# The order of ScalarE's and VectorE's work in a recurrent stage: weight splits ahead of the convolution

## The chip, the core and the metric

The kernel runs on one NeuronCore of a Trainium2 chip (trn2). TensorE multiplies matrices, VectorE and ScalarE do elementwise work, GpSimd some reductions and transfers, SyncE issues most weight transfers. The metric is the device time of one execution in microseconds (us), median over several executions. Lower is better.

## The reference

The model has four residual sub-layers over a sequence of 1024 tokens with 1024 channels: a pooling mixer, a dense MLP, an mLSTM mixer and a second MLP. The change lies in the mLSTM mixer:

```python
proj = jnp.einsum('bsd,de->bse', h, w_in)          # q, k, v, o and two gates
qk = jax.nn.silu(causal_depthwise_conv(qk, conv_w, conv_b))   # 4 taps
...
def mlstm_chunk_step(carry, inp):
    C, n, m = carry
    ...
    s = jnp.einsum('bhtd,bhsd->bhts', q, k) * jnp.exp(log_d - m_out[..., None])
    num = jnp.einsum('bhts,bhsd->bhtd', s, v) + inter[..., None] * jnp.einsum('bhtk,bhkv->bhtv', q, C)
    ...
    C_new = decay[..., None, None] * C + jnp.einsum('bhs,bhsk,bhsv->bhkv', wts, k, v)
...
hs = hs * lax.rsqrt(jnp.mean(hs * hs, axis=-1, keepdims=True) + RMS_EPS)
gated = jax.nn.sigmoid(o_pre) * hs * head_norm_w
return jnp.einsum('bsd,de->bse', gated, w_out)
```

There are 8 heads of 128 channels. Everything is float32.

## The kernel before, in words

**Matmuls in three passes.** Each float32 weight block is split into a high part, rounded to the format that TensorE takes at full rate (`w_hi`, made by ScalarE, `split_hi`, line 1211), and the remainder (`w_lo`, made by VectorE from `raw` and `w_hi`, `split_lo`, line 1739). A product is then three matmuls: high by high, high by low, low by high (lines 778 to 780). The weights and their parts have little room: `raw` holds two blocks, `w_hi` and `w_lo` also two blocks of 1024 columns. So the split of block n overwrites block n - 2, and ScalarE waits in `split_hi` until the projection that used block n - 2 has ended (`group_done`, `BEFORE`), and for the transfer of the raw block. SyncE issues the transfer of block n once block n - 2 is split in both parts.

**The recurrent stage** (755 to 1345 us of the trace) works on the sequence in two halves of 512 tokens, and on the 8 heads in each, 16 steps numbered j = 0 to 15, which are called head 0 to head 15 here. A head has four projections, `("head", j, t)`: q, k, v and the output gate, each 24 matmuls over 512 columns. TensorE's order is written out by hand in `lstm` (line 1074): projection 0 of head j, `turn(j - 1)` (transposes of k and v and the scores, lines 1029 to 1035), projection 1, `updates(j - 1)` (state updates, line 1046), projection 2, `numerators(j - 1)` (lines 1057 and 1061), projection 3, `turn_back(j - 1)` (transposes of the normed head `hnorm`, line 1071). So while head j is projected, head j - 1 is finished. Behind every four heads stands an output product (`second_product`, four blocks), at the start of heads 5, 9 and 13 and at the end.

**ScalarE and VectorE** each have a list of their own, also written by hand (`lstm` at lines 1506 and 2230), and work it off strictly in order; they meet at semaphores. Their pieces, for head j:

- `conv_input(j, t)` (ScalarE, lines 1569 and 1572): moves projection t out of its PSUM bank, scaled into `win` and plain into `craw`. `conv(j, t)` (VectorE, lines 2122 to 2128): the other three taps of the convolution.
- `query(j)` and `keys(j)` (ScalarE, lines 1481 and 1486): silu of the convolution, which makes `qT` and `kT`. `value_copy` (1464) and `output_gate` (1471) move projections 2 and 3.
- `decay_matrix(j - 1)` (ScalarE, 1592, with a load of the exp table): `mx_b`. `by_tokens(j - 1)` (1606 and 1609): `kw` and `v_tok`, which `updates` needs. `rows_to_all(j)` issues two small transfers.
- `probabilities(j - 1)` (VectorE, 2140): `prob`, from the scores and `mx_b`. `states(j - 1)` (2157): three intermediate states `mid`. `rows_for(j)` (2205, 2209). `denominators`, `normalize` (2169 to 2185): `hnorm`. `gate_head` (2194 to 2199).
- `head_squares` and `head_root` (ScalarE, 1619 and 1626).
- `tick(j, part)`: the background work of the slot 4j + part. It runs the normalisations of the layer before or of the other half: squares on ScalarE (1246), sums on VectorE (1799), a reciprocal (1744), residuals (1132 and 1811), normed tiles and their split. `LSTM_SLOTS` says what lies in which slot; heads 1 to 7 and 9 to 15 have the same pattern.
- `BLOCK["head", j, t] + 1` is the block behind projection t of head j: for t = 0 that of projection 1, and so on; for t = 3 that of head j + 1, or of the output product.

Of the kernel before, what the change touches and what calls it, by code (L numbers as in the profile page):

```python
# [20 lines left out]
HEADS = 8  # L21
# [206 lines left out]
def build(nc, x_in, x_tokens, weights, w_first, w_second, vecs_in, consts_in, bands_in, out):  # L228
# [9 lines left out]
    with ExitStack() as ctx:  # L238
# [962 lines left out]
        def _(act):  # L1201
# [286 lines left out]
            def first_head():  # L1488

                split_hi(BLOCK["gate", 0] + 1)  # L1490
                split_hi(BLOCK["head", 0, 0] + 1)
                gates(0)
                split_hi(BLOCK["head", 0, 1] + 1)
                conv_input(0, 0)
                conv_input(0, 1)
                split_hi(BLOCK["head", 0, 2] + 1)
                value_copy(0)
                split_hi(BLOCK["head", 0, 3] + 1)
                gate_weights(0)
                output_gate(0)  # L1500
                query(0)
                keys(0)
                tick(0, 2)
                tick(0, 3)

            def lstm():
                first_head()
                for j in range(1, STEPS + 1):
                    half = j // HEADS
                    g = heads_out(j)  # L1510
                    if g is not None:
                        for b in range(OUT_BLOCKS):
                            split_hi(BLOCK["out", g, b] + 1)
                            if g % 2 == 0:
                                for d in range(2):
                                    out_copy(g, 2 * b + d)
                    if j == STEPS:
                        decay_matrix(j - 1)
                        by_tokens(j - 1)
                        head_norm(j - 1)  # L1520
                        continue
                    if j % HEADS == 0:
                        split_hi(BLOCK["gate", half] + 1)

                    split_hi(BLOCK["head", j, 0] + 1)
                    if j % HEADS == 0:
                        gates(half)
                    if j % HEADS == 1:

                        act.wait_ge(rows_stored, 32 * (half + 1))  # L1530
                        rows_to_all(j - 1)
                    conv_input(j, 0)
                    for f in (by_tokens, decay_matrix) if j % HEADS == 1 else (decay_matrix, by_tokens):
                        f(j - 1)
                    tick(j, 0)
                    split_hi(BLOCK["head", j, 1] + 1)
                    query(j)
                    if j % HEADS:
                        rows_to_all(j)
                    tick(j, 1)  # L1540

                    conv_input(j, 1)
                    split_hi(BLOCK["head", j, 2] + 1)
                    keys(j)
                    value_copy(j)
                    head_squares(j - 1)
                    split_hi(BLOCK["head", j, 3] + 1)
                    head_root(j - 1)
                    tick(j, 2)
                    output_gate(j)  # L1550
                    if j % HEADS == 0:
                        gate_weights(half)
                    tick(j, 3)
                g = STEPS // FT - 1
                for b in range(OUT_BLOCKS):
                    split_hi(BLOCK["out", g, b] + 1)
                for k in range(KT):
                    post_square(5, k)
# [169 lines left out]
        def _(dve):  # L1728
# [487 lines left out]
            def first_head():  # L2216

                split_lo(BLOCK["gate", 0] + 1)
                gates(0)
                split_lo(BLOCK["head", 0, 0] + 1)  # L2220
                split_lo(BLOCK["head", 0, 1] + 1)
                gate_chain(0, lambda: split_lo(BLOCK["head", 0, 2] + 1))
                split_lo(BLOCK["head", 0, 3] + 1)
                conv(0, 0)
                conv(0, 1)
                gate_tail(0)
                tick(0, 2)
                tick(0, 3)

            def lstm():  # L2230
                dve.wait_ge(group_done, STEP[0, STEPS2 - 1][1])
                dve.memset(taps[:, :, :], 0.0)
                dve.memset(zrow[:, :], 0.0)
                dve.memset(m_run[:, 0:1], 0.0)
                dve.memset(rows[:, :], 0.0)
                dve.memset(state[:, :, :], 0.0)
                steps.finish(dve.memset(v_tok[:, :, HEAD_DIM:], 1.0))
                first_head()
                for j in range(1, STEPS + 1):
                    half = j // HEADS  # L2240
                    g = heads_out(j)
                    if g is not None:
                        take_out(g // 2, BLOCK["out", g, 0], GROUPS["out", g, 0], g % 2 == 0)
                    if j == STEPS:
                        probabilities(j - 1)
                        states(j - 1)
                        denominators(j - 1)
                        normalize(j - 1)
                        gate_head(j - 1)
                        continue  # L2250
                    if j % HEADS == 0:
                        split_lo(BLOCK["gate", half] + 1)
                        gates(half)
                    split_lo(BLOCK["head", j, 0] + 1)
                    conv(j, 0)
                    if j % HEADS == 1:
                        gate_columns(half)
                        rows_for(j - 1)
                    probabilities(j - 1)
                    tick(j, 0)  # L2260
                    split_lo(BLOCK["head", j, 1] + 1)
                    if j % HEADS == 0:
                        gate_chain(half, lambda: None)
                    states(j - 1)
                    tick(j, 1)
                    if j % HEADS == 0:
                        split_lo(BLOCK["head", j, 2] + 1)
                    conv(j, 1)
                    if j % HEADS:
                        split_lo(BLOCK["head", j, 2] + 1)  # L2270
                        rows_for(j)
                    denominators(j - 1)
                    split_lo(BLOCK["head", j, 3] + 1)
                    normalize(j - 1)
                    tick(j, 2)
                    gate_head(j - 1)
                    if j % HEADS == 0:
                        gate_tail(half)
                    tick(j, 3)
                g = STEPS // FT - 1  # L2280
                take_out(g // 2, BLOCK["out", g, 0], GROUPS["out", g, 0], g % 2 == 0)
                for k in range(KT):
                    chain_total(k, CHAIN_SUMS[5])
# [129 lines left out]
```

## Time and profile before

| | us |
|---|---|
| median of 3 runs | 2043.67 |
| lowest and highest | 2038.62 and 2045.17 |
| the profiled execution, its own time | 2044.57 |
| its span in the trace | 2042.8 |
| mean granted TensorE clock in it | 0.983 of full |
| TensorE busy in the span | 1950.9 |
| VectorE busy in the span | 1327.6 |
| ScalarE busy in the span | 1055.5 |

The trace is one execution. Matmuls overlap, so the start of one to the start of the next says more than the length of one. In brackets behind an instruction stands the idle time of its engine just before it, and who ended it by the profile; "issue" means that the profile names nobody. DVE is VectorE, ACT is ScalarE, PE is TensorE.

### The profile page before, as it was taken

Reading aid. Unit: us, or ns where it says so; the run is one execution under the profiler, and the core shown is the slowest. Engines: PE = TensorE matmul, PEld = TensorE weight load, DVE = VectorE, ACT = ScalarE, POOL = GpSimd, SP = SyncE. Lnnn points to the kernel's source line nnn. Section 1 sums busy time; section 2 is a strip of 40 time slices with the busy share of each in tenths; the row PEclk is TensorE's granted clock in tenths of the full one; section 3 lists DMA queues with packets and bytes.
Section 4 is the critical chain, followed back from the end, with each engine's and each line's share of the span. In section 5 each row is a group of like instructions: output and inputs, shape, how many; then the busy total and the mean of one; then the engine's idle time right before and its main releaser. Section 6 shows DMA issues by size and latency. Waiting matters only on the chain.

```text
span 2042.8 us, 24561 instructions
## 1 busy us (share of the span) xinstructions
PE 1950.9 (96%) x8652; PEld 1566.0 (77%) x8652; DVE 1327.6 (65%) x2073; ACT 1055.5 (52%) x1793; POOL 91.0 (4%) x121
## 2 busy tenths in 40 slices
PE   9999999998999999999999999899999999899996
PEld 7677788886888787778877778777778888688784
DVE  5675556555766877776767858676555655577765
ACT  6645454553444446766746756453555455344432
POOL 0020000000000200110000100020000000000110
PEclk9999999998999999999999999899999999899998
DMA  5254244349433533343223432243424336833453
GB/s 200 83 165 175 77 156 156 128 172 355 143 93 98 182 114 104 114 145 101 96 73 100 142 117 86 72 154 113 171 83 170 145 139 249 302 93 94 118 176 107
DMA packets 80569, 283.95 MB, mean 139 GB/s; under 512 B 9504, under 2 KB 9632, under 8 KB 73536
## 3 DMA queue, kind: packets, MB, share of 16 engines
q1 hardware_dynamic: 63424, 235.76, 33.1%
q0 software_dynamic: 8320, 27.27, 4.1%
q10 hardware_dynamic: 8704, 19.36, 3.1%
q8 instruction: 70, 1.15, 0.2%
q14 instruction: 51, 0.42, 0.1%
HBM read 213.08 MB, written 69.27 MB: 138 GB/s over the span
## 4 chain that ended last, share of the span: by engine, by line
PE 83%; DVE 6%; DMA 4%; ACT 4%; issue 3%; SPq 0%; POOL 0%; ACTq 0%; DVEq 0%
PE bank L778 7%; PE bank L780 7%; PE bank L779 6%; PE bank L995 4%; PE bank L997 4%; PE bank L996 4%; PE core L946 4%; PE core L947 4%; PE bank L946 4%; PE core L945 4%; PE bank L947 4%; PE bank L945 4%; PE core L995 4%; PE core L997 4%; PE core L996 4%
## 5 line engine op out<-in xcount | busy, mean ns | idle before, releaser
L1739 DVE TENSOR_TENSOR w_lo<-raw,w_hi 128x1024 fp32r<-128x1024 f32 x148 | 186.5, 1262 | 187.9 <-ACT w_hi L1211 185.9
L1211 ACT CAST w_hi<-raw 128x1024 fp32r<-128x1024 f32 x148 | 155.2, 1049 | 190.4 <-PE core L997 56.5
L1388 ACT CAST h_hi<-h_raw 128x512 fp32r<-128x512 f32 x178 | 110.2, 619 | 267.7 <-PE bank L997 112.8
L778 PE MATMUL bank<-x_hi,w_hi 128*128 128x512 f32 x560 | 227.9, 407 | 15.6 <-issue 14.9
L780 PE MATMUL bank<-x_hi,w_lo 128*128 128x512 f32 x560 | 222.2, 397 | 0.0
L779 PE MATMUL bank<-x_lo,w_hi 128*128 128x512 f32 x560 | 221.7, 396 | 0.0
L1988 DVE TENSOR_TENSOR h_lo<-h_raw,h_hi 128x512 fp32r<-128x512 f32 x178 | 122.6, 689 | 122.7 <-ACT h_hi L1388 122.3
L995 PE MATMUL bank<-h_hi,w_hi 128*128 128x512 f32 x424 | 170.9, 403 | 16.8 <-DVE h_lo L1988 16.8
L997 PE MATMUL bank<-h_hi,w_lo 128*128 128x512 f32 x424 | 170.4, 402 | 0.0
L996 PE MATMUL bank<-h_lo,w_hi 128*128 128x512 f32 x424 | 169.3, 399 | 0.0
L995 PE MATMUL core<-h_hi,w_hi 128*128 128x512 f32 x352 | 140.7, 400 | 7.5 <-DVE y L2049 7.5
L997 PE MATMUL core<-h_hi,w_lo 128*128 128x512 f32 x352 | 140.9, 400 | 0.0
L996 PE MATMUL core<-h_lo,w_hi 128*128 128x512 f32 x352 | 140.4, 399 | 0.0
L778 PEld LDWEIGHTS bank<-x_hi,w_hi 128*128 128x128 f32 x560 | 105.7, 189 | 42.7 <-issue 20.0
L1883 DVE TENSOR_TENSOR w_lo<-sums,w_hi 128x512 fp32r<-128x512 f32 x96 | 66.2, 690 | 101.5 <-ACT w_hi L1239 98.8
L780 PEld LDWEIGHTS bank<-x_hi,w_lo 128*128 128x128 f32 x560 | 105.5, 188 | 25.6
L779 PEld LDWEIGHTS bank<-x_lo,w_hi 128*128 128x128 f32 x560 | 105.6, 189 | 24.1 <-issue 1.0
L878 PE MATMUL bank<-x_hi,w_hi 128*128 128x512 f32 x256 | 105.1, 410 | 9.3 <-ACT y_part L1284 4.5
L995 PEld LDWEIGHTS bank<-h_hi,w_hi 128*128 128x128 f32 x424 | 81.4, 192 | 38.4 <-issue 10.2
L2027 DVE TENSOR_TENSOR w_lo<-w,w_hi 128x512 fp32r<-128x512 f32 x136 | 97.4, 716 | 9.4 <-ACT w_hi L1404 4.8
L1174 POOL PARTITION_ALL_REDUCE tot<-acc x10 | 34.5, 3454 | 1532.0 <-DVEq L1803 1532.0
L880 PE MATMUL bank<-x_hi,w_lo 128*128 128x512 f32 x256 | 101.7, 397 | 0.0
(314 smaller groups left out, 4487.1 us busy)
## 6 DMA issues: line engine op xcount, KB each, us to landing
raw<-weights SPq DMA_DIRECT2D x148, 512.0 KB, 3.4
h_pair_dram<-y SPq DMA_DIRECT2D x24, 1792.0 KB, 6.7
h_raw<-h_pair_dram SPq DMA_DIRECT2D x168, 256.0 KB, 2.8
w<-second_pairs SPq DMA_DIRECT2D x32, 768.0 KB, 8.1
x_scratch<-y POOLq DMA_DIRECT2D x48, 256.0 KB, 2.4
raw_odd<-first_pairs SPq DMA_DIRECT2D x12, 1024.0 KB, 7.3
raw<-first_pairs SPq DMA_DIRECT2D x12, 1024.0 KB, 7.1
xold<-x_scratch POOLq DMA_DIRECT2D x40, 256.0 KB, 3.6
```

Source lines behind the costliest of these rows:

```text
L778: nc.tensor.matmul(o, a, hi(t), start=(k == 0), stop=False)
L779: nc.tensor.matmul(o, a, lo(t), start=False, stop=False)
L780: last = nc.tensor.matmul(o, b, hi(t), start=False, stop=(k == n - 1))
L945: nc.tensor.matmul(o, a, xh[:, k, :], start=(fresh and k == 0), stop=False, skip_group_check=True)
L946: nc.tensor.matmul(o, a, xl[:, k, :], start=False, stop=False, skip_group_check=True)
L947: last = nc.tensor.matmul(o, b, xh[:, k, :], start=False, stop=(final and k == 3), skip_group_check=True)
L995: nc.tensor.matmul(o[:, :], a, hh, start=(fresh and first), stop=False, skip_group_check=True)
L996: nc.tensor.matmul(o[:, :], a, hl, start=False, stop=False, skip_group_check=True)
L997: ins = nc.tensor.matmul(o[:, :], b, hh, start=False, stop=(final and last), skip_group_check=True)
L1211: nc.scalar.copy(w_hi[:, ROW[u] * T:(ROW[u] + 2) * T], raw[:, (n % RAW) * BLK:(n % RAW + 1) * BLK]).then_inc(hi_ready, 1)
L1739: dve.tensor_tensor(w_lo[:, s], raw[:, (n % RAW) * BLK:(n % RAW + 1) * BLK], w_hi[:, s].bitcast(F32), ALU.subtract).then_inc(lo_ready, 1)
L1988: dve.tensor_tensor(lo, h_raw[:, at % H_RAW, :], hi.bitcast(F32), ALU.subtract).then_inc(h_lo_ready, 1)
```

## The change

In both lists, of ScalarE and of VectorE, the split of the block of projection 2 moves ahead of `conv_input(j, 0)` and `conv(j, 0)`, and that of projection 3 ahead of `conv_input(j, 1)` and `conv(j, 1)`: each stands at the place where the projection that held its rows has ended. The background work of the last slot, `tick(j, 3)`, moves from the end of head j to behind the split of projection 1 of head j + 1. On ScalarE `by_tokens` now comes ahead of `decay_matrix` in every head (before only where j % 8 = 1). In ScalarE's and VectorE's list:

```diff
@@ first_head() @@
                 tick(0, 2)
-                tick(0, 3)
@@ ScalarE, lstm() @@
                     if j == STEPS:
+                        tick(j - 1, 3)
                         decay_matrix(j - 1)
...
+                    tick(j - 1, 3)
+                    split_hi(BLOCK["head", j, 1] + 1)
                     conv_input(j, 0)
-                    for f in (by_tokens, decay_matrix) if j % HEADS == 1 else (decay_matrix, by_tokens):
-                        f(j - 1)
+                    by_tokens(j - 1)
+                    decay_matrix(j - 1)
                     tick(j, 0)
-                    split_hi(BLOCK["head", j, 1] + 1)
                     query(j)
                     if j % HEADS:
                         rows_to_all(j)
                     tick(j, 1)
 
+                    split_hi(BLOCK["head", j, 2] + 1)
                     conv_input(j, 1)
-                    split_hi(BLOCK["head", j, 2] + 1)
                     keys(j)
...
-                    tick(j, 3)
@@ VectorE, lstm() @@
                     split_lo(BLOCK["head", j, 0] + 1)
+                    tick(j - 1, 3)
+                    split_lo(BLOCK["head", j, 1] + 1)
                     conv(j, 0)
                     if j % HEADS == 1:
                         gate_columns(half)
                         rows_for(j - 1)
                     probabilities(j - 1)
                     tick(j, 0)
-                    split_lo(BLOCK["head", j, 1] + 1)
                     if j % HEADS == 0:
                         gate_chain(half, lambda: None)
                     states(j - 1)
                     tick(j, 1)
-                    if j % HEADS == 0:
-                        split_lo(BLOCK["head", j, 2] + 1)
+                    split_lo(BLOCK["head", j, 2] + 1)
                     conv(j, 1)
                     if j % HEADS:
-                        split_lo(BLOCK["head", j, 2] + 1)
                         rows_for(j)
...
-                    tick(j, 3)
```

TensorE's list is the same in both kernels.

On VectorE, in head 3, from `probabilities` on; `-` is the kernel before, `+` the changed one:

```order
 L2140 SCALAR_TENSOR_TENSOR prob<-core,mx_b 128x512
 L1744 RECIPROCAL rstd<-tot 128x512
-L1739 TENSOR_TENSOR w_lo<-raw,w_hi 128x1024
 L2157 SCALAR_TENSOR_TENSOR mid<-state,inter_b,core 128x129
 L2157 SCALAR_TENSOR_TENSOR mid<-mid,inter_b,core 128x129 x2
 L1132 SCALAR_TENSOR_TENSOR step_t<-y,vecs,rstd 128x512
 L1811 TENSOR_TENSOR y<-xold,step_t 128x512
-L2122 COPY craw<-taps 128x16
-L2123 COPY taps<-craw 128x16
-L2128 SCALAR_TENSOR_TENSOR win<-craw,vecs,win 128x512 x3
-L1739 TENSOR_TENSOR w_lo<-raw,w_hi 128x1024
+L1739 TENSOR_TENSOR w_lo<-raw,w_hi 128x1024
```

The first w_lo (projection 2) has moved up ahead of the first convolution, which ends just above this piece; the second one (projection 3) now stands ahead of the second convolution, whose three lines follow it in the changed kernel.

On ScalarE, in head 3, from `conv_input(3, 0)` to `query(3)`; the split of projection 2 now stands ahead of this piece:

```order
 L1569 ACTIVATE win<-bank,vecs 128x512
 L1572 COPY craw<-bank 128x512
+L1606 ACTIVATE kw<-core,cols 128x128 x4
+L1609 COPY v_tok<-core 128x4x128
 L1592 ACT_TABLE_LOAD
 L1592 ACTIVATE mx_b<-mx_b,cols 128x128 x4
-L1606 ACTIVATE kw<-core,cols 128x128 x4
-L1609 COPY v_tok<-core 128x4x128
-L1211 CAST w_hi<-raw 128x1024
 L1481 ACT_TABLE_LOAD
```

The split has left its place behind v_tok, and kw and v_tok stand ahead of the exp table and mx_b.

On VectorE, behind head 4, where four blocks of the output product and two of head 5 are split; acc is the sum of the background work of slot 19:

```order
 L2199 TENSOR_TENSOR hid_lo<-relu_sq,hid_hi 128x512
+L1739 TENSOR_TENSOR w_lo<-raw,w_hi 128x1024 x5
 L1799 TENSOR_TENSOR acc<-acc,sq 128x512 x2
-L1739 TENSOR_TENSOR w_lo<-raw,w_hi 128x1024 x5
+L1739 TENSOR_TENSOR w_lo<-raw,w_hi 128x1024
```

The two sums stood ahead of five splits and now stand behind them, ahead of the split of projection 2 of head 5.

## Rows read from the trace of the kernel before

**Rows 1.** The page, part 1: busy us (share of the span) and instructions of each engine

```profile
PE 1950.9 (96%) x8652; PEld 1566.0 (77%) x8652; DVE 1327.6 (65%) x2073; ACT 1055.5 (52%) x1793; POOL 91.0 (4%) x121
```

**Rows 2.** Waits of 755 to 1345 us: in total, times, longest us

```profile
PE bank L778 <- issue: 17.9, 18, 2.4
...
PE core L1071 <- DVE hnorm L2185: 5.8, 2, 4.4
```

**Rows 3.** Timeline, TensorE: start us, us, engine line op out<-in [idle before <-releaser]

```profile
858.83 0.47 PE L778 MATMUL bank<-x_hi,w_hi 128*128 128x512 f32 x1 [1.04 <-issue]
...
896.58 0.47 PE L778 MATMUL bank<-x_hi,w_hi 128*128 128x512 f32 x1 [1.83 <-issue]
...
909.54 0.48 PE L778 MATMUL bank<-hid_hi,w_hi 128*128 128x512 f32 x1 [1.07 <-issue]
```

**Rows 4.** Timeline, TensorE: first matmuls of lines 1029 and 1071, heads 3, 4, 6

```profile
849.38 0.60 PE L1029 MATMUL core<-consts,kT 128*128 128x128 f32 x4
...
871.89 0.60 PE L1071 MATMUL core<-consts,hnorm 128*128 128x128 f32 x4
...
877.93 0.60 PE L1029 MATMUL core<-consts,kT 128*128 128x128 f32 x4
...
902.27 0.60 PE L1071 MATMUL core<-consts,hnorm 128*128 128x128 f32 x4
...
960.14 0.60 PE L1029 MATMUL core<-consts,kT 128*128 128x128 f32 x4
...
981.38 0.60 PE L1071 MATMUL core<-consts,hnorm 128*128 128x128 f32 x4
```

**Rows 5.** Timeline, ScalarE, head 3

```profile
849.58 0.78 ACT L1569 ACTIVATE win<-bank,vecs 128x512 f32<-128x512 f32 x1 [2.46 <-PE bank L780]
...
850.85 1.28 ACT L1592 ACT_TABLE_LOAD   x1
852.14 1.28 ACT L1592 ACTIVATE mx_b<-mx_b,cols 128x128 f32<-128x128 f32 x4
853.33 0.60 ACT L1606 ACTIVATE kw<-core,cols 128x128 f32<-128x128 f32 x2
...
854.80 1.07 ACT L1211 CAST w_hi<-raw 128x1024 fp32r<-128x1024 f32 x1
...
864.07 0.63 ACT L1486 ACTIVATE kT<-win 128x512 f32<-128x512 f32 x1 [4.17 <-DVE win L2128]
```

**Rows 6.** Timeline, VectorE, head 3

```profile
853.52 0.69 DVE L2140 SCALAR_TENSOR_TENSOR prob<-core,mx_b 128x512 f32<-128x512 f32 x1
854.13 3.34 DVE L1744 RECIPROCAL rstd<-tot 128x512 f32<-128x512 f32 x1
857.51 1.22 DVE L1739 TENSOR_TENSOR w_lo<-raw,w_hi 128x1024 fp32r<-128x1024 f32 x1
858.65 0.34 DVE L2157 SCALAR_TENSOR_TENSOR mid<-state,inter_b,core 128x129 f32<-128x129 f32 x1
...
859.80 0.75 DVE L1132 SCALAR_TENSOR_TENSOR step_t<-y,vecs,rstd 128x512 f32<-128x512 f32 x1
...
861.42 0.17 DVE L2122 COPY craw<-taps 128x16 f32<-128x16 f32 x1
```

**Rows 7.** Timeline, head 8: ScalarE's kT and TensorE's line 1071

```profile
1041.45 0.63 ACT L1486 ACTIVATE kT<-win 128x512 f32<-128x512 f32 x1 [9.92 <-DVE win L2128]
...
1047.77 0.66 PE L1071 MATMUL core<-consts,hnorm 128*128 128x128 f32 x4 [1.39 <-DVE hnorm L2185]
```

**Rows 8.** Timeline: two waits. Windows behind them: us, busy by engine, granted clock, DMA

```profile
483.32 0.77 PE L995 MATMUL bank<-h_hi,w_hi 128*128 128x512 f32 x1 [2.53 <-DVE h_lo L1988]
...
1343.87 0.47 PE L878 MATMUL bank<-x_hi,w_hi 128*128 128x512 f32 x1 [2.63 <-ACT w_hi L1211]
...
483.30:486.70 3.40, 3.38 (x9) 2.75 (x10) 1.77 (x3) 1.14 (x2) 0.00 (x0) 0.56 1.05 448
1343.87:1347.30 3.43, 3.43 (x15) 2.79 (x16) 3.43 (x2) 1.69 (x4) 3.43 (x3) 1.00 0.46 153
```

More of the change, by code:

```diff
@@ L2227, in first_head @@
                 tick(0, 2)
-                tick(0, 3)
             def lstm():
@@ L2254, in lstm @@
                     split_lo(BLOCK["head", j, 0] + 1)
+                    tick(j - 1, 3)
+                    split_lo(BLOCK["head", j, 1] + 1)
                     conv(j, 0)
```

## The prediction

> **What bounds the kernel.** I read the page first: TensorE is busy for 1950.9 of 2042.8 us, VectorE for 1327.6 [rows 1]. Only TensorE's idle time can be won, and the change moves no TensorE instruction. The waits inside the recurrent stage (755 to 1345 us) come next: TensorE waited 17.9 us in 18 waits ahead of line 778, the first matmul of a projection, and 5.8 us ahead of line 1071, the turning back of a head [rows 2]. "Issue" there stands for a wait that the profile gives to nobody; the timeline names it. In head 3 the third projection starts at 858.83, 1.04 us late, and the low half of its weights (w_lo) was written from 857.51 to 858.73 [rows 3, 6]. So TensorE waits for VectorE's half of the split. The same holds ahead of the fourth projection of head 4 (1.83 us) and of the second output block (1.07 us) [rows 3].
>
> A head is best measured from its first transposing matmul (line 1029; I call this moment S) to its first matmul of line 1071. Head 6 takes 981.38 - 960.14 = 21.24 us without any wait; head 3 takes 22.51 and head 4 takes 24.34 [rows 4]. So head 3 loses 1.27 us for a recorded wait of 1.04, and head 4 loses 3.10. By the same subtraction (head 1 and 9 have 0.44 more work) heads 1, 2, 5, 6, 7 lose 2.6, 2.1, 0.8, 0 and 0.7, and heads 9 to 15 lose 1.2, 2.1, 1.3, 3.1, 0.9, 0, 0.7. Together 19.9 us, and the first and third output phase another 2.5. That is all that the change can reach: 22.4 us, or 1.1%.
>
> **The hidden competitor.** Line 1071 waits for hnorm, which ScalarE and VectorE make in turn: keys (kT), the copy of v, four squares, the next w_hi, the root with its table load, then VectorE's scaling. In head 8, where this chain ended last, it ran from kT at 1041.45 to line 1071 at 1047.77, 6.32 us [rows 7]. So TensorE waits there as soon as kT starts later than S + 21.24 - 6.32 = S + 14.9. kT starts when the convolution of k (line 2128) ends. In head 3 of the old kernel that was 864.07 = S + 14.69 [rows 5, 4]: 0.2 us to spare. The chain is nearly as long as TensorE's work already.
>
> **The change, walked for head 3 (S = 849.38).** ScalarE. It starts 0.20 after S as before [rows 4, 5]. First now w_hi, 1.07 long, to S + 1.28; then win and craw, 1.27 (849.58 to 850.85), to 2.54; kw and v_tok, 1.5, to 4.1; the exp table 1.28 and mx_b 1.28, to 6.8 [rows 5]. By the old order mx_b ended at 853.42 = S + 4.0. VectorE's w_lo of the third projection comes at S + 1.4 to 2.5 instead of 8.1 to 9.3, and TensorE needs it at S + 8.2: **the 1.04 us wait goes.** The raw block had landed long before: ScalarE has taken it after its own work in every head, not after a transfer.
>
> VectorE then does the first convolution (2.65) to S + 5.3 and stands at prob, which waits for mx_b: 1.5 us of VectorE idle time that was not there. prob ends at 7.4; the reciprocal takes 3.38 (854.13 to 857.51), to 10.8; the states 1.15, to 12.0; step_t and y 1.6, to 13.6 [rows 6]. Now w_lo of the fourth projection, 1.14 (857.51 to 858.65), comes ahead of the second convolution and not behind it, to 14.7; the convolution, 2.65 (861.42 to 864.07), ends at S + 17.4 [rows 5, 6]. TensorE could begin line 1071 at 21.24; kT's chain gives 17.4 + 6.3 = 23.7. **The wait comes back ahead of line 1071 as 2.5 us in one piece, where 1.27 was lost: head 3 becomes 1.2 us longer.**
>
> The other heads by the same steps, with their own background work between them (tick, which the change leaves in each place except the last slot of a head):
> - Heads 2 and 10: the squares of the last slot now wait for VectorE's sums, which stand behind w_lo. The third block's w_hi starts 1.8 us after S, four sums follow, kT at S + 17.9: 3.0 against 2.1 lost, +0.9 each.
> - Heads 4 and 12: prob to 7.4, one sum and one residual to 9.5, states to 10.7, two sums and two residuals to 15.3, w_lo to 16.4, convolution to 19.1: 4.2 lost (0.9 ahead of the fourth projection, 3.2 ahead of line 1071) against 3.1, +1.1 each.
> - Heads 3 and 11: +1.2 each.
> - Heads 5, 7, 13, 15: little on VectorE between prob and the convolution; kT at S + 13.6 to 14.9, no wait. -0.8 and -0.7, twice.
> - Heads 6 and 14: normed tiles, kT at S + 15.3, +0.35 each. Head 1 and 9: +0.1 and +0.2, since kw and mx_b stand behind the gate columns. Head 8: its long gate chain on VectorE starts 0.4 earlier, -0.4.
> - Output blocks after heads 4 and 12: the last slot's squares and sums no longer stand ahead of their split: the waits (1.07 in the first [rows 3], 1.43 in the third phase) go, -2.5.
>
> Sum: +6.4 (heads 2 to 4, 10 to 12), +1.0 (1, 6, 9, 14), -3.0 (5, 7, 13, 15), -0.4, -2.5 = **+1.5 us**. Bounds: -22.4, if nothing waits ahead of line 1071, to +6, if each loaded head is 0.8 worse than walked. SP's queue gains by it, since blocks are released earlier; the two row transfers of ScalarE's queue are issued at the same place between query and tick. The moved last slot is hidden behind a projection everywhere but in heads 2 and 10.
>
> **The clock.** Seven waits of 2.5 to 3.2 us in one piece (heads 1 to 4, 10 to 12) replace waits that were mostly below 2 us. After the wait of 2.53 us at 483.32 the granted clock was 0.56, mostly the 1.2 GHz level; after 2.63 us at 1343.87 it stayed at 1.00, the 2.4 GHz level [rows 8]. The first stretch did 9 matmuls in 3.40 us, the second 15 in 3.43, so nine need 2.06 at full clock: a fall costs 1.35. The bounds are no fall, 0, and seven, +9.5. I take four, +5.4: one of the two rows fell, and all seven waits are about as long as these or longer.
>
> The Trainium skill (TensorE: Matmul & The Clock Gate, "A second HAM failure mode: psum-queue depth-cycling") says that frequent short idle spells between groups of matmuls are enough to make the clock swing. The rows agree in part: one wait of two was followed by the fall; by the page the seven would all be, and the sum 4 us higher.
>
> **Total.** 2044.57 (this execution) + 1.5 + 5.4 = 2051.5; the execution lay 0.9 above the median of the runs shown, 2043.67. Against the median: 2050.6, rounded **2051**.
>
> **The rivals.**
> - *The gain stays.* The weights wait goes and line 1071 doesn't take its place, because VectorE finds time I don't see. Time: 2043.67 - 0.7 x 22.4 = 2028, from the point on where kT starts before S + 15 in the loaded heads. For it: all 18 waits are ahead of weights. Against it: 0.2 us to spare in head 3 and the new idle time ahead of prob. The Trainium skill (Perfetto Trace Analysis, "Optimization Strategy") would have one find the gap on the engine that matters and make what it waits for start sooner, which is this edit; by that rule alone the time is that of this rival. The trace speaks against: the gap has a second condition 0.2 us behind the first.
> - *The waits move, the clock holds.* +1.5 alone, or a little less: 2043 to 2046. For it: 2.63 us without a fall [rows 8].
> - *The clock falls after each long wait* and loaded heads are worse than walked: 2043.67 + 1.5 + 9.5 + 2 = 2057, clearly slower. For it: 2.53 us with a fall, and by the page above this is the case that would come.
> - *The change does nothing:* the split can't start earlier since its raw block isn't there. 2043.7. Against: in the old head 3 ScalarE's idle time of 2.46 ahead of win ended with a projection, not with a transfer [rows 5].
>
> **How the numbers follow.** About 0.3% (6.1 us) is what a measurement of this kernel can tell from no change. The forecast has 0.50: waits moved, two to six falls, 2048 to 2054, three fifths of it above 2049.8. The gain that stays has 0.15 (faster), the clock that holds 0.18 (same), falls everywhere 0.12 (slower), nothing 0.05 (same). Slower 0.30 + 0.12 = 0.42; same 0.20 + 0.18 + 0.05 = 0.43; faster 0.15. The range 2040 to 2057 leaves out the gain that stays and the end of the worst case.
>
> **What would show it.** Right: the idle time ahead of line 778 in the stage falls from 17.9 to under 5 us; that ahead of line 1071 rises from 5.8 to about 20, released by VectorE's hnorm; prob waits for mx_b in most heads; in head 3 kT starts near S + 17.4; more stretches at half clock between 800 and 1300. Wrong: heads 3 and 11 at 21.3 us from S to line 1071, or kT before S + 15 in them; then VectorE wasn't the queue that decides, and the time is near 2028.

## The result and the profile after

The changed kernel takes 2051.29 us (median of 7 runs, 2049.99 to 2054.85), the kernel before 2044.1 us (2038.62 to 2048.46, 7 runs): a ratio of 1.0036 with a 95% interval of 1.0025 to 1.0048. It is slower by some 7 us, a third of a per cent. The forecast was 2051 us, with a range of 2040 to 2057. The profiled execution of the changed kernel spans 2049.6 us, that of before 2042.8: +6.8, so the traces show the whole difference.

The page after, part 1, with the columns of [rows 1]:

```profile
PE 1953.1 (95%) x8652; PEld 1568.3 (77%) x8652; DVE 1325.1 (65%) x2073; ACT 1054.5 (51%) x1793; POOL 91.2 (4%) x121
```

As many instructions as before on each engine. TensorE is busy for 2.2 us more with the same matmuls, which is a first sign of a lower clock. The waits of the changed kernel between 755 and 1350 us, the view of [rows 2]: in total, times, longest:

```profile
PE core L1071 <- DVE hnorm L2185: 25.9, 10, 4.4
DVE prob L2140 <- ACT mx_b L1592: 21.8, 14, 3.2
...
PE bank L778 <- issue: 3.6, 4, 1.2
```

The wait for weights has gone from 17.9 to 3.6 us, and the wait for hnorm has come in its place, 5.8 to 25.9. VectorE's prob, which waited for mx_b once in the old kernel (3.2 us), does so in 14 heads. Head 3 shows both on TensorE's timeline of the changed kernel, with heads 4 and 6 beside it as in [rows 4]:

```profile
851.96 0.60 PE L1029 MATMUL core<-consts,kT 128*128 128x128 f32 x4
...
875.50 0.99 PE L1071 MATMUL core<-consts,hnorm 128*128 128x128 f32 x4 [2.14 <-DVE hnorm L2185]
...
883.17 0.60 PE L1029 MATMUL core<-consts,kT 128*128 128x128 f32 x4
...
900.23 0.47 PE L778 MATMUL bank<-x_hi,w_hi 128*128 128x512 f32 x1 [1.24 <-issue]
...
909.00 0.66 PE L1071 MATMUL core<-consts,hnorm 128*128 128x128 f32 x4 [2.94 <-DVE hnorm L2185]
...
966.32 0.60 PE L1029 MATMUL core<-consts,kT 128*128 128x128 f32 x4
...
987.56 0.60 PE L1071 MATMUL core<-consts,hnorm 128*128 128x128 f32 x4
```

Head 6 still takes 21.24 us. Head 3 takes 23.54 where it took 22.51 [rows 4], head 4 25.83 where it took 24.34. The chain behind it in head 3, on ScalarE's timeline and then VectorE's:

```profile
852.21 1.05 ACT L1211 CAST w_hi<-raw 128x1024 fp32r<-128x1024 f32 x1 [3.08 <-PE bank L780]
...
857.85 0.68 ACT L1592 ACTIVATE mx_b<-mx_b,cols 128x128 f32<-128x128 f32 x2
...
869.18 0.64 ACT L1486 ACTIVATE kT<-win 128x512 f32<-128x512 f32 x1 [6.61 <-DVE win L2128]
```

```profile
853.30 1.23 DVE L1739 TENSOR_TENSOR w_lo<-raw,w_hi 128x1024 fp32r<-128x1024 f32 x1 [3.55 <-ACT w_hi L1211]
...
858.63 0.69 DVE L2140 SCALAR_TENSOR_TENSOR prob<-core,mx_b 128x512 f32<-128x512 f32 x1 [1.56 <-ACT mx_b L1592]
859.24 3.34 DVE L1744 RECIPROCAL rstd<-tot 128x512 f32<-128x512 f32 x1
...
865.39 1.23 DVE L1739 TENSOR_TENSOR w_lo<-raw,w_hi 128x1024 fp32r<-128x1024 f32 x1
...
866.82 2.32 DVE L2128 SCALAR_TENSOR_TENSOR win<-craw,vecs,win 128x512 f32<-128x512 f32 x3
```

With S = 851.96, w_lo of the third projection is ready at S + 2.6 instead of 9.4 [rows 6]. VectorE idles 1.56 us ahead of prob. kT starts at S + 17.2 where it started at S + 14.7 [rows 5], and line 1071 follows at S + 23.5, 6.32 us behind kT, which is the length that the chain had in head 8 of the old kernel [rows 7].

The clock is the second half of the loss. These windows of the changed kernel (us; busy time by engine; granted clock as a share of full speed; DMA share; GB/s) are the 3.4 us ahead of two falls of the clock, which take in most of the wait, with the stretches behind them, and then the other two stretches:

```profile
810.70:814.10 3.40, 1.61 (x7) 0.95 (x6) 3.02 (x11) 2.21 (x3) 0.00 (x0) 1.00 0.12 22
814.10:817.50 3.40, 2.93 (x9) 2.54 (x10) 2.61 (x6) 2.28 (x3) 0.00 (x0) 0.52 0.38 133
872.10:875.50 3.40, 1.26 (x6) 0.69 (x5) 3.08 (x11) 3.35 (x5) 0.00 (x0) 1.00 0.24 41
875.50:878.90 3.40, 3.40 (x11) 2.82 (x12) 2.97 (x5) 2.26 (x4) 1.07 (x2) 0.53 0.49 188
909.70:913.10 3.40, 3.40 (x10) 2.63 (x9) 2.97 (x5) 3.37 (x4) 0.55 (x1) 0.52 0.28 107
1053.00:1056.40 3.40, 3.40 (x11) 2.82 (x12) 1.87 (x3) 3.33 (x5) 0.00 (x0) 0.53 0.27 104
```

Ahead of the first two falls TensorE is busy for 1.6 and 1.3 us and the clock is full; then it is busy for 2.9 to 3.4 us and the clock is at the 1.2 GHz level. What a fall costs where it stands can be read from the time from line 1071 of one head to line 1029 of the next. It is 6.04 us in the old kernel, 6.10 behind a long wait without a fall, and 7.50 and 7.67 behind the falls at 814.1 and 875.5: **1.4 and 1.6 us each**. Not all of it is lost for good, as the kernel with the filled wait will show. The trace of before has one such stretch between the first head and the last, in head 8, and it cost nothing there:

```profile
1039.20:1042.60 3.40, 3.40 (x9) 2.62 (x9) 2.40 (x4) 1.15 (x3) 0.00 (x0) 0.50 0.48 154
```

TensorE had to wait 1.39 us for hnorm a little later [rows 7]. In the changed kernel the same place is reached at full clock and the wait is 2.94 us, with the fall behind it. The half clock had only filled the wait.

The account, from line 1029 of the first head to line 1071 of head 15 (505.42 us before, 511.74 after):

| part | forecast | measured |
|---|---|---|
| heads 1 to 7, 9 to 15 | +4.4 | +3.8 (lost 19.8 before, 23.6 after) |
| head 8 | -0.4 | -0.4 (26.77, 26.38) |
| output phases | -2.5 | -2.8 |
| half-clock stretches | +5.4 | +5.4 (four) |
| small gaps | 0 | +0.3 |
| sum | +6.9 | +6.3 |

The output phases and the half-clock stretches overlap in time. They are told apart by the same places in the kernel with the filled wait below, where the clock never falls: the first output phase takes 28.50 us there and 30.03 here, the second 29.60 and 30.49. So two of the four falls cost 1.5 and 0.9.

Of the 0.5 us that are missing to the span's 6.8, 0.8 lie ahead of this stretch and -0.3 behind it.

### The profile page after: what moved, and what is told of

It is laid out like the page before. It is cut to its first block and busy times, and to the rows that moved or that the text cites. A ratio compares the mean times of both kernels' runs of the same rounds, so it can differ in the third digit from the quotient of the medians.

```text
span 2049.6 us, 24559 instructions
## 1 busy us (share of the span) xinstructions
PE 1953.1 (95%) x8652; PEld 1568.3 (77%) x8652; DVE 1325.1 (65%) x2073; ACT 1054.5 (51%) x1793; POOL 91.2 (4%) x121
## 5 line engine op out<-in xcount | busy, mean ns | idle before, releaser
L780 PEld LDWEIGHTS bank<-x_hi,w_lo 128*128 128x128 f32 x560 | 105.7, 189 | 25.6
```

The costliest lines, as they stand in the source:

```text
L780: last = nc.tensor.matmul(o, b, hi(t), start=False, stop=(k == n - 1))
```

## The experiments

My theory: the early third split is a gain, the parts that make VectorE and ScalarE later ahead of the second convolution take it back, and waits of over 2 us in one piece, which bring the clock down, make a loss of it. The rivals: the early split itself is bad; the clock has no part in it; a single part carries all. Each of the change's four parts was run alone. Then come four combinations of them, two kernels that hold the clock up, and one that takes out a disturbance. Ratios are against the kernel before on the same chip.

### The third split alone

The kernel before with only the third split moved:

```diff
+                    split_hi(BLOCK["head", j, 1] + 1)
                     conv_input(j, 0)
...
-                    split_hi(BLOCK["head", j, 1] + 1)
@@ VectorE @@
+                    split_lo(BLOCK["head", j, 1] + 1)
                     conv(j, 0)
...
-                    split_lo(BLOCK["head", j, 1] + 1)
```

> The kernel before with one part of the change: the split of projection 2's block ahead of conv_input(j, 0) and conv(j, 0); all else in the old places. Theory (VectorE's queue is the second condition, and what fills it too early is the other two parts): mx_b is not put off by by_tokens, so prob ends at S + 5.9 in head 3 and kT starts at S + 14.7, within the 14.9 allowed; the wait ahead of projection 2 goes and little comes back. Lost in the heads 1, 2, 3, 4: 2.1, 0, 0.4, 2.9 us instead of 2.6, 2.1, 1.3, 3.1. Time about 10 us below the kernel before: 2034. Rival (any earlier split is paid back ahead of line 1071, because ScalarE and VectorE have no room at all in the loaded heads): 2043 to 2048, with 10 us or more of waits ahead of line 1071.

Measured: 2035.97 us, ratio 0.9961 [0.9941, 0.9980]. Head 3 on its TensorE, ScalarE and VectorE timelines:

```profile
847.26 0.60 PE L1029 MATMUL core<-consts,kT 128*128 128x128 f32 x4
...
868.70 0.60 PE L1071 MATMUL core<-consts,hnorm 128*128 128x128 f32 x4
```

```profile
851.03 1.28 ACT L1592 ACTIVATE mx_b<-mx_b,cols 128x128 f32<-128x128 f32 x4
...
861.82 0.63 ACT L1486 ACTIVATE kT<-win 128x512 f32<-128x512 f32 x1 [3.98 <-DVE win L2128]
```

```profile
852.41 0.69 DVE L2140 SCALAR_TENSOR_TENSOR prob<-core,mx_b 128x512 f32<-128x512 f32 x1
```

With mx_b made first, prob comes at S + 5.2 without a wait (S + 6.7 in the changed kernel), kT at S + 14.6, and head 3 takes 21.44 us: 0.20 lost. The gain of the change is real, 8 us, and it is in this part. One detail missed: head 2 was to lose nothing and loses 1.46 us. GpSimd's sum over partitions (829.78 to 833.04) stands beside its second convolution in the trace, and one small copy of the convolution takes 2.10 us instead of 0.17; the last section comes back to this.

### The fourth split alone

The kernel before with only the fourth split moved:

```diff
+                    split_hi(BLOCK["head", j, 2] + 1)
                     conv_input(j, 1)
-                    split_hi(BLOCK["head", j, 2] + 1)
@@ VectorE @@
-                    if j % HEADS == 0:
-                        split_lo(BLOCK["head", j, 2] + 1)
+                    split_lo(BLOCK["head", j, 2] + 1)
                     conv(j, 1)
...
-                        split_lo(BLOCK["head", j, 2] + 1)
```

> The kernel before with one part: the split of projection 3's block ahead of conv_input(j, 1) and conv(j, 1). Theory: it puts the convolution of k and so kT 1.14 us later in every head; waits ahead of the fourth projection (1.83 and 0.73 us) go and come back ahead of line 1071, as 0.6 us more in heads 2 and 10 and 0.5 more in 4 and 12. Time 2 us above the kernel before, up to 5 with a clock fall: 2046. Rival (the early fourth split is the useful part): 2039 or less.

Measured: 2049.04 us, ratio 1.0016 [1.0002, 1.0031], +3.3 us. The heads lose 22.45 instead of 19.82 us: heads 2, 4, 10 and 12 0.6 to 0.7 more each, the others as before. It puts 1.2 us of w_lo ahead of the convolution that kT waits for. A small loss by itself, just clear of the noise.

### The decay steps in the old order

The changed kernel with only their order undone:

```diff
-                    by_tokens(j - 1)
-                    decay_matrix(j - 1)
+                    for f in (by_tokens, decay_matrix) if j % HEADS == 1 else (decay_matrix, by_tokens):
+                        f(j - 1)
```

> The changed kernel with decay_matrix ahead of by_tokens again, as in the kernel before. Theory: VectorE no longer stands idle ahead of prob, prob comes 1.5 us sooner; the waits ahead of line 1071 shrink by 1.5 us in heads 3 and 11, by 1.0 in 4 and 12, by nothing in 1, 2 and 10 (there the squares on ScalarE decide), and one or two falls of the clock go: 2044, 7 us below the changed kernel. Rival (the order of these two is nothing, the 1.07 us of the earlier w_hi and the w_lo ahead of the second convolution do it all): within 1 us of the changed kernel, 2051.

Measured: 2043.33 us, ratio 0.9985 [0.9968, 1.0002]: 10 us less than the changed kernel. The heads lose 18.02 instead of 23.60 us, head 3 0.79 instead of 2.30, and two of the four falls are gone. This swap of two small steps is the most expensive part of the change.

### The wait filled

The changed kernel with 8 matmuls of 512 columns ahead of the wait for hnorm in heads 1 to 4, 8 and 10 to 12; nothing reads their sums:

```diff
             def turn_back(j):
+                pe.wait_ge(state_ready, j + 1)
+                if j in (0, 1, 2, 3, 7, 9, 10, 11):
+                    xh = XH((j + 1) // HEADS, 0)
+                    for _ in range(8):
+                        nc.tensor.matmul(core[0][:, :], xh[:, 0:P], xh, start=True, stop=True)
                 pe.wait_ge(hnorm_ready, j + 1)
 
-                pe.wait_ge(state_ready, j + 1)
```

> The changed kernel with 8 more matmuls of 512 columns (1.9 us) on TensorE ahead of line 1071 in heads 1 to 4, 8 and 10 to 12, into a bank that is written over; they fill the wait for hnorm and feed nothing. Theory (four falls of the clock, each 1.4 to 1.6 us, are most of the loss): the waits of 2.1 to 2.9 us stay, filled, the granted clock stays at its upper level from 800 to 1300 us, and the time falls by 4 to 6 us to 2046. Rival (the falls cost nothing, since the other engines decide the pace of the stage): 2051 or, with the added work, more.

Measured: 2046.6 us, ratio 1.0012 [0.9994, 1.0030], 4.9 us less than the changed kernel. Head 3 on its TensorE timeline, and the window from line 1029 of the first head to that of the last, first of this kernel and then of the changed one:

```profile
873.47 2.00 PE L1070 MATMUL core<-x_hi 128*128 128x512 f32 x8
875.77 0.66 PE L1075 MATMUL core<-consts,hnorm 128*128 128x128 f32 x4 [0.31 <-DVE hnorm L2189]
```

```profile
791.19:1300.28 509.09, 495.68 (x2458) 407.90 (x2457) 366.70 (x702) 327.28 (x601) 29.99 (x36) 1.00 0.34 109
```

```profile
790.91:1304.31 513.40, 486.43 (x2394) 400.85 (x2393) 367.09 (x702) 327.31 (x601) 30.02 (x36) 0.99 0.34 108
```

64 more matmuls, TensorE 9.3 us longer busy, and the stretch 4.3 us shorter: no half-clock stretch is left in it. hnorm is no earlier in head 3; only the speed behind the wait has changed. By the intervals the 4.9 us are just clear of the noise. The other executions say the same: the mean granted clock of one has a median of 0.984 over the twelve runs here, and of 0.980 over the seven of the changed kernel. This shows the clock's part.

It also shows that the four falls cost 4.3 us on balance, less than the 5.4 they cost where they stand. Head 2 on TensorE's timeline, first of this kernel, then of the changed one, where the clock had fallen just ahead of it:

```profile
820.92 0.60 PE L1029 MATMUL core<-consts,kT 128*128 128x128 f32 x4
...
846.13 0.66 PE L1075 MATMUL core<-consts,hnorm 128*128 128x128 f32 x4 [1.10 <-DVE hnorm L2189]
```

```profile
822.07 0.60 PE L1029 MATMUL core<-consts,kT 128*128 128x128 f32 x4
...
845.87 0.66 PE L1071 MATMUL core<-consts,hnorm 128*128 128x128 f32 x4 [2.38 <-DVE hnorm L2185]
```

25.21 us here and 23.80 there. While TensorE was slow ahead of head 2, ScalarE and VectorE got on with their lists, so the fall of 1.4 us was given back as a shorter wait. So a fall cost nothing lasting here, where TensorE had to wait for hnorm again soon, nor in head 8 of the old kernel.

### The last slot alone

The kernel before with only the background slot moved:

```diff
+                    tick(j - 1, 3)
                     conv_input(j, 0)
...
-                    tick(j, 3)
```

(and the same ahead of `conv(j, 0)` on VectorE; at both ends of the stage the slot moves as in the change).

> Only the last slot's tick, tick(j, 3), is moved behind the head's end; the splits and the order of the two decay steps stay as before. My account: the waits around the output blocks go (-3.4 us) and heads 4, 7, 12 and 15 lose the small waits that the slot caused (-1.4 us together), while in heads 2 and 10 the squares of the moved slot stand ahead of the fourth split's upper half and put it off (+1.6 us each). Sum +1.4 from nothing gives about 2043 us, against 2044.7 before. Rival 1: the moved slot moves nothing, 2044.7. Rival 2: the slot was the cause of most of the waits in the loaded heads, and the time falls by 5 us, to 2039.

Measured: 2044.92 us, ratio 1.0009 [1.0000, 1.0017]: +1.8 where I expected about -1.6 (that is the sum of -3.4, -1.4 and twice +1.6; the "+1.4" above is a slip). The output waits went as expected (28.43 us twice from line 1071 to the next line 1029 in the first and third output phase, before 29.75 and 30.10). Heads 2 and 10 lose 2.1 us more each instead of 1.6, and it is their third split that is late, not the fourth. The third projection of head 2 and the fourth of head 4:

```profile
829.59 0.71 PE L778 MATMUL bank<-x_hi,w_hi 128*128 128x512 f32 x1 [2.39 <-issue]
...
897.47 0.47 PE L778 MATMUL bank<-x_hi,w_hi 128*128 128x512 f32 x1 [1.83 <-issue]
```

The wait of head 2 is 0.84 us in the old kernel and 2.39 here; that of head 4 is 1.83 in both. The clock fell behind both rows and behind the like wait of head 10, near 1119.8; the old kernel has no fall at these places. In this trace the heads lose 25.6 us instead of 19.8, and a half-clock stretch of 6.8 us makes the second output phase 2.1 us longer. That is more than the first and third output phase win.

### The decay steps swapped alone

The kernel before with by_tokens ahead of decay_matrix in every head:

```diff
-                    for f in (by_tokens, decay_matrix) if j % HEADS == 1 else (decay_matrix, by_tokens):
-                        f(j - 1)
+                    by_tokens(j - 1)
+                    decay_matrix(j - 1)
```

> Only the order of the two decay steps is changed: by_tokens stands ahead of decay_matrix in every head. My account: prob then waits 1.5 to 2.7 us for ScalarE's exponential while VectorE stands idle, and everything behind it on VectorE, the third and fourth split among it, is later by as much. Heads 3 and 11 lose 1.5 us more each, 2 and 10 0.9, 4 and 12 1.7, so about 2052 us with nothing given back. Rival: VectorE has room there, nothing changes, 2044.7.

Measured: 2066.59 us, ratio 1.0111 [1.0098, 1.0124]: **+23 us, nearly three times what I expected.** Heads 2 and 3 on its TensorE and VectorE timelines:

```profile
831.12 0.67 PE L778 MATMUL bank<-x_hi,w_hi 128*128 128x512 f32 x1 [2.99 <-issue]
...
863.40 0.47 PE L778 MATMUL bank<-x_hi,w_hi 128*128 128x512 f32 x1 [3.21 <-ACT w_hi L1211]
```

```profile
858.09 0.69 DVE L2140 SCALAR_TENSOR_TENSOR prob<-core,mx_b 128x512 f32<-128x512 f32 x1 [2.22 <-ACT mx_b L1592]
858.70 3.34 DVE L1744 RECIPROCAL rstd<-tot 128x512 f32<-128x512 f32 x1
862.08 1.23 DVE L1739 TENSOR_TENSOR w_lo<-raw,w_hi 128x1024 fp32r<-128x1024 f32 x1
```

In this kernel, as in the old one, the third w_lo stands behind prob and the reciprocal, so 2.2 us of waiting there arrive at TensorE at once: 3.21 us where it waited 1.04 [rows 3]. Heads 6, 7, 14 and 15, which have little background work, lose 0.7 to 1.5 us more too, which I had put at nothing, and there are five stretches at half clock, two of them 6.8 us long, against one of 3.4. The heads lose 42.5 us instead of 19.8.

### The swap with an early third split

The third split alone, with the swap added (the two diffs above together):

> The early third split (alone 2036 us) with by_tokens ahead of decay_matrix in every head; slot and fourth split as before. With the late third split the swap of the decay steps alone cost 23 us, where I expected 8: third and fourth projections waited up to 3.2 us. My account now: the swap delays whatever VectorE does behind prob, and with the early third split only the fourth projection is left there to be late, so the cost falls to about 8 to 10 us, 2044 to 2046. Rival 1: the cost of the swap does not depend on where the third split stands: 2058. Rival 2: the early split hides it wholly: 2036.

Measured: 2042.88 us, ratio 1.0000 [0.9989, 1.0011]: against the third split alone (0.9961) the swap costs 8 us here, and 23 with the late split. So the early third split hides two thirds of the swap's cost, and the swap takes back all that the early split wins.

### Third split and slot, and the slot where it pays

Two kernels: the third split and the moved slot together, and the same with the slot moved in heads 1, 4, 5 and 7 of each eight only. The second on ScalarE; VectorE's list is changed alike:

```diff
+                    if (j - 1) % HEADS in (0, 3, 4, 6):
+                        tick(j - 1, 3)
+                    split_hi(BLOCK["head", j, 1] + 1)
                     conv_input(j, 0)
...
-                    tick(j, 3)
+                    if j % HEADS not in (0, 3, 4, 6):
+                        tick(j, 3)
```

> The early third split (measured alone at 0.996 of before) and the moved last slot together, with the fourth split and the decay steps as before. My account: the early third split gives 2036, the moved slot takes another 3.0 us at the output blocks and 1.4 in heads 4, 7, 12 and 15, and gives 2.1 back in heads 2 and 10: about 2033.7 us. Rival: the two hide the same waits and the pair gives no more than the third split alone, 2036.

> As the kernel with the early third split and the moved slot, but the slot is moved in heads 1, 4, 5 and 7 of each eight only, where an output block or a small wait stands behind it, and stays in place in the others, so the fourth split of heads 2 and 10 is not put off. My account: about 2032.5 us. Rival: the waits at the output blocks are not what costs, and it stays at 2036.

Measured: 2036.45 us, ratio 0.9967 [0.9955, 0.9980], and 2034.25 us, ratio 0.9960 [0.9946, 0.9973]. Against the third split alone (0.9961) neither differs by more than the intervals. In the first, heads 2 and 10 lose 0.6 to 0.7 us more, as expected; the first and third output phase are shorter by 1.3 and 0.7. The expected 2 to 3 us can't be seen in the times. The rival of 2036 fits the first. The second lies between its forecast of 2032.5 and its rival of 2036, and the noise can't part them.

### The best of these, with the clock held

The last kernel with 8 unread matmuls ahead of the fourth projection of heads 4 and 12 and, as in the filled kernel above, ahead of the wait for hnorm in head 8. The first of the two places:

```diff
+                        if t == 3 and j in (4, 12):
+                            for _ in range(8):
+                                nc.tensor.matmul(core[0][:, :], XH(half, 0)[:, 0:P], XH(half, 0), start=True, stop=True)
                         if j < STEPS:
                             project(("head", j, t), BLOCK["head", j, t], half)
```

> The kernel with the early third split and the slot moved in four of eight heads (2034 us), with 8 matmuls of 512 columns, whose sums nobody reads, ahead of the fourth projection of heads 4 and 12 and ahead of the wait for hnorm in head 8: the three waits behind which its trace shows the clock at half. My account: three stretches at half clock go, 1.5 us each, so 2029 to 2031 us. Rival: the matmuls cost what they save, or the clock falls elsewhere: 2034.

Measured: 2030.63 us, ratio 0.9938 [0.9926, 0.9951], **12.7 us less than before**, as expected. Against the same kernel without these matmuls it is some 4 us less, which is just clear of the noise. Between 755 and 1280 us no half-clock stretch is left (granted clock, 1.00, stands third from the end):

```profile
755.00:1280.00 525.00, 517.16 (x2555) 426.95 (x2554) 388.85 (x744) 344.02 (x621) 29.99 (x36) 1.00 0.35 111
```

### GpSimd's sums left out

The changed kernel with the four sums over partitions of this stage replaced by a constant. The sums are left out, so its results are not those of the model:

```diff
+                if n in GONE:
+                    pool.memset(tot[:, :], 64.0 * D).then_inc(tot_ready, 1)
+                    return
                 nc.gpsimd.partition_all_reduce(tot[:, :], acc[:, :], P, RADD).then_inc(tot_ready, 1)
```

> The changed kernel with the four sums over partitions that GpSimd makes in this stage left out (tot is set to a constant instead, so the background chain is scaled wrongly). In the traces of before and after, the VectorE instruction that starts while GpSimd sums takes 1.80 to 2.39 us for w_lo instead of 1.22, and 2.10 instead of 0.17 for the copy of the taps. My account: GpSimd's sum holds VectorE up; without it w_lo takes 1.22 us in all heads, heads 2 and 10 lose some 1.2 us less each, and the time is about 2049 us. Rival: the stretch has another cause (the transfers at that time), the rows stay at 2.39 and 1.8 and the time at 2051.3.

Measured: 2046.89 us, ratio 1.0019 [1.0009, 1.0030], 3.5 us less than the changed kernel by the ratios. Every w_lo of the stage takes 1.21 to 1.23 us; in the changed kernel four take 1.80 to 2.39. Head 10 loses 2.83 us instead of 3.97, and my forecast of it had been 3.0. The other 2 us or so can't be given to the sums: the falls lie elsewhere in this trace (near 844, 1049, 1161 and 1196; four again), and the clock isn't the same in every execution. The mean granted clock of the changed kernel's seven runs goes from 0.978 to 0.983; one stretch of 3.4 us at half clock is 0.0008 of it, so by my estimate the number of such stretches differs by several between runs of one kernel.

## Why the prediction held, and where it didn't

- **The wait comes back ahead of line 1071 (right).** Forecast for heads 1 to 4 were losses of 2.7, 3.0, 2.5 and 4.2 us; measured 2.42, 2.56, 2.30 and 4.59. Heads 5 and 7 were forecast to lose nothing and lose 0.01 each. Head 3 fits step by step: idle ahead of prob 1.5 forecast, 1.56 measured; kT at S + 17.4, measured S + 17.2; loss +1.2, measured +1.03. The subtraction that gave S + 14.9 as the latest harmless start of kT was the step that decided, and the third split alone bears it out: kT at S + 14.6, and TensorE doesn't wait there. (Heads 1 and 9 don't have the 0.44 us more work that the prediction names: TensorE does 112 matmuls from S to line 1071 in every head. The losses were taken without it, so no sum changes.)
- **Heads 2 and 10 (+0.9 each; measured +0.5 and +1.9).** Head 10's extra 1.1 us is GpSimd's sum over partitions, which I had not priced; without it the loss was 2.83. Head 2 meets the same sum, but there a fall of the clock at 814.1 had given ScalarE and VectorE 1.46 us more ahead of S. The filled kernel has the sum and no fall, and its head 2 loses 3.97 too.
- **Heads 6 and 14 (+0.35 each; measured 0.0).** I had kT at S + 15.3; in head 6 it starts at S + 14.9 (981.18), just in time by the subtraction.
- **Output phases (-2.5; measured -2.8).** Right. The slot alone shows that this gain does not come by itself: the same move lengthened waits in heads 2 and 10, and the clock fell there.
- **The clock (four falls, 5.4 us; measured four, 5.4 where they stand and 4.3 on balance).** The price of 1.35 us per fall was the mean of what was measured (1.4, 1.6, 1.5 and 0.9); that part of it is given back later was not in the sum. That it came to four was luck: two rows can't give such a number. Eight waits, not seven, came in one piece of 2.1 to 2.9 us: the eighth is head 8's, which a half-clock stretch had covered in the trace of before. Four of the eight were followed by a fall. The rule from the Trainium skill that I weighed there (TensorE: Matmul & The Clock Gate, "A second HAM failure mode: psum-queue depth-cycling"), read as a fall after each, would have given twice as many.
- **The whole.** Without the clock the forecast was +1.5; the filled kernel, which has no fall, is 2.0 us longer from the first head to line 1071 of head 15 than the old one (507.41 and 505.42). So both halves of the sum hold within about 1 us, on one trace each. That the total came within 0.3 us is luck: the executions of the changed kernel differ by 5 us among themselves.
- **The signs named beforehand** all came: 3.6 us ahead of line 778 (under 5), 25.9 ahead of line 1071 (about 20), prob waiting for mx_b in 14 heads, more half-clock stretches.
- **What the prediction didn't see:** the change is not one thing. By the ratios, adding its parts one after another gives -8.0 us (third split), +1.2 (slot), +3.7 (fourth split), +10.4 (the decay steps swapped). The first and the last are clear of the noise; of the two between, each lies within it. I had walked all four at once and got the sum right, and so did not notice that one part is a gain of 8 us. The rival in which the gain stays, 2028 us, is nearly reached by the third split, the slot where it pays and the clock held up together: 2030.63. Its rule (the Trainium skill, Perfetto Trace Analysis, "Optimization Strategy") is to make what TensorE waits for start sooner. By the runs that was right for the third split, -8 us alone, and not for the fourth, +3.3 alone, though TensorE had waited for both.

## What to carry over

Measure the longest harmless delay of the second condition before removing the first: here TensorE waited for weights, and the normalization chain stood 0.2 us behind. An edit that moves several steps should be run part by part, since a gain of 8 us and a loss of 10 looked like one small loss. Look at the length of single waits and not only at their sum: behind waits under 2 us the clock fell once in 18 cases, behind those of 2 to 3.5 us in 27 of 48. Where a long wait can't be removed, matmuls that nobody reads can pay for themselves: 5 us in one kernel here and some 4 in another.

## What was not expected of the hardware

**A sum on GpSimd holds up VectorE.** GpSimd's sum over partitions in the changed kernel, the w_lo that VectorE starts just behind it, and the same w_lo in the kernel without the sums (line 1744 there):

```profile
833.67 3.23 POOL L1174 PARTITION_ALL_REDUCE tot<-acc  x1 [120.04 <-DVEq L1803]
```

```profile
834.61 2.38 DVE L1739 TENSOR_TENSOR w_lo<-raw,w_hi 128x1024 fp32r<-128x1024 f32 x1 [1.09 <-ACT w_hi L1211]
```

```profile
833.70 1.23 DVE L1744 TENSOR_TENSOR w_lo<-raw,w_hi 128x1024 fp32r<-128x1024 f32 x1 [1.08 <-ACT w_hi L1216]
```

The instruction takes 2.38 us, without the sum 1.23. In head 5 of the changed kernel another w_lo starts later in a sum and is stretched less:

```profile
947.15 3.23 POOL L1174 PARTITION_ALL_REDUCE tot<-acc  x1 [35.37 <-DVEq L1803]
```

```profile
948.65 1.82 DVE L1739 TENSOR_TENSOR w_lo<-raw,w_hi 128x1024 fp32r<-128x1024 f32 x1
```

In the trace of before, the copy of the taps starts 0.21 us after a sum:

```profile
831.89 3.26 POOL L1174 PARTITION_ALL_REDUCE tot<-acc  x1 [119.06 <-DVEq L1803]
```

```profile
832.10 2.10 DVE L2123 COPY taps<-craw 128x16 f32<-128x16 f32 x1
```

This copy takes 0.17 or 0.18 us elsewhere. The Trainium skill (SBUF — State Buffer, "SBUF: two separate sides") says that VectorE and GpSimd share a pair of ports as an exclusive lock: a VectorE instruction with two SBUF inputs or in a two-port mode, and a GpSimd instruction, block each other, and the one that started first keeps the pair for its whole length. The three rows agree with a lock, but not with the whole length. Take from each end the time that the instruction needs alone: 836.99 - 1.23 = 835.76, 950.47 - 1.23 = 949.24, 834.20 - 0.17 = 834.03. Each lies 1.1 us ahead of the end of the sum as the profile has it (836.90, 950.38, 835.15). So VectorE is let go 1.1 us before the recorded end. The same subtraction gives 1.13 to 1.14 us in all 90 cases of the 13 traces in which a VectorE instruction is stretched beside such a sum. Whether GpSimd gives the ports back so early or the profile ends the sum too late isn't shown. Not every instruction is stretched: the three of line 2157, one input of which is in PSUM, take 0.35 us each inside the sum of 947.15, as elsewhere.

**The fall is a matter of chance near these lengths.** In the 13 traces of this study, between 755 and 1285 us, the clock fell within a few us of 1 of 18 waits of 1.5 to 2 us of TensorE, of 7 of 18 of 2 to 2.5, of 20 of 30 of 2.5 to 3.5, and of both longer ones. One and the same wait, 2.93 or 2.94 us ahead of line 1071, was followed by a fall in heads 4 and 8 of the changed kernel and by none in heads 10 and 12. What decides between them stays open.
